# A recurrent branch run as four streams (direction x half of the heads) instead of two directions

## The reference, cut to what matters

```python
def step(s, inp):
    r_t, w_t, k_t, v_t, a_t, b_t = inp
    sa = jnp.einsum("bhvk,bhk->bhv", s, a_t)
    s = (s * w_t[:, :, None, :] + sa[..., None] * b_t[:, :, None, :]
         + v_t[..., None] * k_t[:, :, None, :])
    return s, jnp.einsum("bhvk,bhk->bhv", s, r_t)
...
for d in range(N_DIR):
    a_d = a[:, :, d]
    k_d = heads(k * (1 + (a_d - 1) * k_a))
    y_d, s_d = wkv_scan(rh, heads(decay[:, :, d]), k_d, vh, -kk, kk * heads(a_d),
                        s0[:, d].astype(f32), reverse=(d == 1))
```

## Time and profile before

| | us |
|---|---|
| median of 3 runs | 1853.98 (1853.29 to 1858.33) |
| span of the profiled execution (no other time of its own is given) | 1866.7 |
| PE matmul busy | 1767.0 (95%) |
| DVE busy | 1136.2 (61%) |
| ACT busy | 887.2 (48%) |
| POOL busy | 579.5 (31%) |

### The profile page before, as it was taken

The page is one execution under the profiler, slowest core; times in us unless marked ns, Lnnn a source line. Parts: engine busy times, 40 slices in busy tenths (PEclk is TensorE's granted clock), DMA queues, the critical chain, the costliest instruction groups (busy, mean ns, idle before and its releaser), DMA issues.

```text
span 1866.7 us, 40944 instructions
## 1 busy us (share of the span) xinstructions
PE 1767.0 (95%) x16496; PEld 1617.0 (87%) x16496; DVE 1136.2 (61%) x1650; ACT 887.2 (48%) x1338; POOL 579.5 (31%) x438
## 2 busy tenths in 40 slices
PE   7999989899999999999999799999989999999996
PEld 7888868799999999999888698999878888888885
DVE  1675657655222121004766787542499999999998
ACT  2562132153444334335532423433557777777775
POOL 1651000154666666565530002655510000000000
PEclk9999969999999999999999899999999999999998
DMA  8534241433443344343342500335579999999991
GB/s 283 172 102 148 94 139 54 151 99 104 136 124 105 122 136 134 125 120 102 91 136 90 178 26 22 119 101 161 203 250 345 335 348 338 331 329 325 326 342 45
DMA packets 226886, 321.62 MB, mean 172 GB/s; under 512 B 15798, under 2 KB 169780, under 8 KB 226612
## 3 DMA queue, kind: packets, MB, share of 16 engines
q1 hardware_dynamic: 220112, 308.26, 50.4%
q0 software_dynamic: 1728, 6.29, 0.9%
q10 hardware_dynamic: 4900, 4.93, 0.8%
HBM read 315.77 MB, written 3.67 MB: 171 GB/s over the span
## 4 chain that ended last, share of the span: by engine, by line
PE 76%; DVE 13%; issue 5%; ACT 2%; DMA 2%; POOL 1%; DVEq 1%; SPq 0%; ACTq 0%
PE bank L630 74%; DVE e_w_rest L189 4%; PE bank L627 2%; DMA ring<-in_w_ada 2%; DVE S L2103 2%; POOL weights_rest L2520 1%; DVE cvT L2052 1%; DVE yacc L2410 1%; DVE esig L2469 1%; ACT weights_rounded L1416 0%; ACT e_w_rounded L1453 0%; DVE U L2133 0%; DVE ey_rest L2424 0%; DVE St L2155 0%; DVE hT L1863 0%
## 5 line engine op out<-in xcount | busy, mean ns | idle before, releaser
L2520 POOL TENSOR_TENSOR weights_rest<-ring,weights_rounded 128x512 fp32r<-128x512 f32 x344 | 467.8, 1366 | 482.1 <-ACT weights_rounded L1416 481.8
L1416 ACT ACTIVATE weights_rounded<-ring 128x512 fp32r<-128x512 f32 x344 | 213.6, 629 | 332.7 <-PE bank L630 328.6
L1453 ACT ACTIVATE e_w_rounded<-e_raw 128x1024 fp32r<-128x1024 f32 (+1 forms) x327 | 315.7, 989 | 101.4 <-PE bank L630 96.2
L189 DVE TENSOR_TENSOR e_w_rest<-e_raw,e_w_rounded 128x1024 fp32r<-128x1024 f32 (+1 forms) x326 | 355.1, 1133 | 8.5 <-ACT e_w_rounded L1453 7.6
L630 PE MATMUL bank<-h_rounded,weights_rounded 128*128 128x384 f32 x688 | 235.7, 343 | 8.4 <-POOL weights_rest L2520 5.7
L630 PE MATMUL bank<-h_rounded,weights_rest 128*128 128x384 f32 x688 | 233.2, 339 | 0.0
L630 PE MATMUL bank<-h_rest,weights_rounded 128*128 128x384 f32 x688 | 232.0, 337 | 0.0
L630 PE MATMUL bank<-e_w_rounded,hG_rounded 128*128 128x512 f32 (+1 forms) x432 | 166.6, 386 | 13.0 <-DVE e_w_rest L189 6.9
L630 PE MATMUL bank<-e_w_rounded,hG_rest 128*128 128x512 f32 (+1 forms) x432 | 162.5, 376 | 0.0
L630 PE MATMUL bank<-e_w_rest,hG_rounded 128*128 128x512 f32 (+1 forms) x432 | 162.5, 376 | 0.0
L2603 POOL DMA_INDIRECT hgt<-h_rows,rows_at x9 | 13.6, 1515 | 449.1 <-DVE wnext L2439 449.1
(11 more groups left out here) (355 smaller groups left out, 3658.7 us busy)
## 6 DMA issues: line engine op xcount, KB each, us to landing
ring<-in_w_ada SPq DMA_DIRECT2D x96, 512.0 KB, 6.1
e_raw<-in_moe_w_down SPq DMA_DIRECT2D x90, 512.0 KB, 4.6
ring<-in_w_in SPq DMA_DIRECT2D x88, 512.0 KB, 4.6
e_raw<-in_moe_w_gate SPq DMA_DIRECT2D x72, 512.0 KB, 7.1
e_raw<-in_moe_w_up SPq DMA_DIRECT2D x72, 512.0 KB, 8.0
e_raw<-in_moe_w_gate SPq DMA_DIRECT2D x36, 384.0 KB, 6.4
e_raw<-in_moe_w_up SPq DMA_DIRECT2D x36, 384.0 KB, 4.3
ring<-in_ffn_w_gate SPq DMA_DIRECT2D x22, 512.0 KB, 4.8
```

What stands on the lines that cost most here:

```text
L189: eng.tensor_tensor(wl, e_raw[n % E_RAW][:, 0:kn * w], wr.bitcast(F32), ALU.subtract).then_inc(s("e_rest"), 1)
L1416: a(w_parts[n % NSLOT][0], raw, ACT.Copy).then_inc(*E.up("rounded_ready", *key))
L1453: a(e_w[n % E_PARTS][0][:, 0:kn * w], e_raw[n % E_RAW][:, 0:kn * w], ACT.Copy).then_inc(s("e_rounded"), 1)
L2520: pool.tensor_tensor(wl, raw, wr.bitcast(F32), ALU.subtract).then_inc(*E.up("rest_ready", *key))
```

## The change

The branch runs as four streams s = 2 d + g, where g is a half of the heads (heads 4 g to 4 g + 3, channel tiles 2 g and 2 g + 1).

- PE, ACT and DVE get a `scan` that takes work to run behind W, in front of the wait for U, and behind the step. Scan 0 carries the levels of stream 1; scan 1 the tokens, pairs, level 0 and levels 1 and 2 of stream 2; scan 2 the same of stream 3; scan 3 has ada halves and taps. The levels' units are now 8 and 4 blocks (`UNITS`), each with its own bank (3 and 7) and its own Xs.
- `low` products of direction 1 run between the levels of stream 0. Keys of direction 1 are prepared per half (`later_decay(g)`, `later_keys(g)`, `grown_keys(g)`, `later_queries(g)`, ACT's `later_exps(g)`).
- The state is kept without the zeros; products with it take one row half, then wait for PE's own semaphore, then the other (`with_state`). The two chunks of a step are updated by one add and one multiply over two neighbouring banks (`two`). `Sfin` is a slot of `St`.
- Outputs of a chunk pair follow as soon as its chunks are scanned (`done_pairs`).
- W and U share bank 0; there is one `Wb`.
- AR and BK no longer fit beside each other with both directions alive: BK lies over x, the decays of direction 1 (`incl1`, `excl1`) over h. x and h are written to DRAM at the head of the z stage by ACT's queue and read back in stream 3's last levels; DVE waits for them in front of BK, of the rest of h and of the residual.
- No `FILL` matmuls; `meanwhile` runs ada halves alone. Taps: 12 ahead of the first masks, the others as below.

```diff
+UNITS = ((0, 8), (8, 4))
...
                 def meanwhile(n):

                     for _ in range(n):
-                        if next(next_ada, None) is None:
-                            for _ in range(FILL):
-                                mm(psum[7][:, 0:P], ident, ident, True, True)
+                        next(next_ada, None)
...
+                def with_state(b, s_, cs, k):
+
+                    d, g = divmod(s_, 2)
+                    for hh in range(2):
+                        for mm_ in range(2):
+                            for c in cs:
+                                if c != starts(d)[0]:
+                                    hr = hh ^ (c % 2)
+                                    m, h4, r = 2 * g + mm_, 2 * mm_ + hr, quads[hr]
+                                    last = mm(b[quads[c % 2], h4 * C:(h4 + 1) * C], AR[r, m, c, k, :], St[r, c + 1, m, :],
+                                              False, hh == 1 and mm_ == 1)
+                        if hh == 0:
+                            last.then_inc(*E.step())
+                            pe.wait_ge(*E.latest())
+                    return last
...
+                def scan(s_, after_w, before_s, after_s):
+
+                    d = s_ // 2
+                    for i in range(len(steps(d))):
+                        step_w(s_, i)
+                        after_w[i]()
+                        step_u(s_, i)
+                        if nxt(d, steps(d)[i][-1]) is None:
+                            before_s[i]()
+                            pe.wait_ge(*drained("U", l, s_, i))
                         else:
...
+                            for part, _ in enumerate(step_s(s_, i)):
+                                if part == 0:
+                                    before_s[i]()
+                        if done_pairs(d)[i] is not None and i + 1 < len(steps(d)):
+                            outputs(s_, done_pairs(d)[i])
+                        after_s[i]()
...
+                level_d(0, 5)
+                meanwhile(1)
+                scan(0, [lambda lev=lev: level_x(1, lev) for lev in range(1, 5)], [lambda lev=lev: level_d(1, lev) for lev in range(1, 5)],
+                     [lambda: meanwhile(1), nothing, nothing, nothing])
+                level_x(1, 5)
+                ending(0)
+                level_d(1, 5)
...
+                    scan(s_ - 1, [keyed, lambda: pairs(s_, 1, (3, 7)), lambda: level_x(s_, 1), lambda: level_x(s_, 2)],
+                         [stated, nothing, lambda: level_d(s_, 1), lambda: level_d(s_, 2)],
+                         [paired, lambda: pairs(s_, 2, (3, 7)), nothing, nothing])
+                    level_x(s_, 3)
+                    ending(s_ - 1)
+                    level_d(s_, 3)
+                    for lev in (4, 5):
+                        meanwhile(1)
+                        level_x(s_, lev)
+                        meanwhile(1)
+                        level_d(s_, lev)
+                    meanwhile(3 - s_)
+                one = lambda: meanwhile(1)
+                scan(3, [one] * 4, [nothing] * 4, [one, one, nothing, nothing])
+                ending(3)
                 for _ in next_ada:
                     pass
-                meanwhile(3)
```

ACT, and DVE behind the first keys:

```diff
+                act.dma_start(x_keep, xT).then_inc(*E.up("x_kept", l, by=16))
+                act.dma_start(h_keep, hT).then_inc(*E.up("h_kept", l, by=16))
...
+                scan(0, [lambda lev=lev: squares_of(1, lev) for lev in range(1, 5)], [nothing] * 4,
+                     [lambda: key_gain(1, (0, 1)), lambda: (key_gain(1, (2, 3)), later_exps(0)), lambda: later_exps(1), nothing])
...
+                first_keys()
+                taps(12)
+                for cp in range(NCP):
+                    masks(0, cp)
+                level_0(0)
...
+                scan(0, [nothing] * 4,
+                     [lambda: (level(1, 1), later_decay(1)), lambda: (level(1, 2), later_keys(0)),
+                      lambda: (level(1, 3), grown_keys(0)), lambda: level(1, 4)])
+                level(1, 5)
+                for s_ in (2, 3):
+                    later_queries(s_ - 2)
+                    scan(s_ - 1, [nothing] * 4,
+                         [lambda: masks(s_, 0), lambda: (masks(s_, 1), masks(s_, 2), level_0(s_)),
+                          lambda: level(s_, 1), lambda: level(s_, 2)])
+                    level(s_, 3)
+                    outputs(s_ - 1, done_pairs(0 if s_ == 2 else 1)[-1])
+                    if s_ == 2:
+                        later_keys(1)
+                    else:
+                        taps(3)
+                    level(s_, 4)
+                    if s_ == 2:
+                        grown_keys(1)
+                    else:
+                        taps(3)
+                    level(s_, 5)
+                    taps(2)
+                scan(3, [nothing] * 4, [lambda: taps(4)] * 4)
+                taps(2 * CONV_W)
+                outputs(3, done_pairs(1)[-1])
+                dve.wait_ge(*E.latest())
+                dve.wait_ge(*at("h_back", l))
                 for g in range(4):
                     rest("gate", l, g, hT[:, 2 * g:2 * g + 2, :])
```

More of the change, by code:

```diff
@@ L18 @@
 C = 64
+NG = NH // 2
 NC_ = T // C
@@ L49 @@
 F32 = mybir.dt.float32
-FILL = 4
 F32R = mybir.dt.float32r
@@ new lines, in step_w @@
+                def step_w(s_, i):
+                    d, g = divmod(s_, 2)
+                    b = begin("W", l, s_, i, use=0)
+                    for h4 in range(NG):
+                        for c in steps(d)[i]:
+                            cp, q = chunk(c)
+                            h = NG * g + h4
+                            mm(b[q, h4 * C:(h4 + 1) * C], S1[q, nth(s_, cp, h4), 2 * C:3 * C], vtok[q, cp, h * C:(h + 1) * C],
+                               h4 == 0, c == starts(d)[0] and h4 == NG - 1)
+                    if i == 0:
+                        pe.wait_ge(*drained("s0", l, s_))
+                    else:
+                        pe.wait_ge(*drained("S", l, s_, i - 1, 0))
+                    with_state(b, s_, steps(d)[i], 0).then_inc(*E.fill("W", l, s_, i))
@@ new lines, in step_u @@
+                def step_u(s_, i):
+                    d = s_ // 2
+                    b = begin("U", l, s_, i, use=0)
+                    if i == 0:
+                        for w in range(len(UNITS)):
+                            pe.wait_ge(*drained("D", l, s_, LEVELS, w))
+                    for h4 in range(NG):
+                        for c in steps(d)[i]:
+                            cp, q = chunk(c)
+                            last = mm(b[q, h4 * C:(h4 + 1) * C], Tt[q, nth(s_, cp, h4), :], Wb[q, h4 * C:(h4 + 1) * C], True, True)
+                    last.then_inc(*E.fill("U", l, s_, i))
@@ new lines, in into_state @@
+                def into_state(s_, i, k, values, start):
+                    d, g = divmod(s_, 2)
+                    step = steps(d)[i]
+                    for mm_ in range(2):
+                        for hh in range(2):
+                            for j, c in enumerate(step):
+                                cp, q = chunk(c)
+                                hr = hh ^ (c % 2)
+                                h4 = 2 * mm_ + hr
+                                h = NG * g + h4
+                                last = mm(bank("S", l, s_, i, j)[quads[hr], mm_ * C:(mm_ + 1) * C], tok[q, k, cp, h * C:(h + 1) * C],
+                                          values(q, c, h4), start and mm_ == 0, not start and mm_ == 1)
+                                if not start and mm_ == 1 and hh == 1:
+                                    last.then_inc(*E.fill("S", l, s_, i, j))
@@ new lines, in _ @@
+                first_state(0, 2)
+                for cp in range(NCP):
+                    tokens(1, cp, (3, 7, 0)[cp])
+                first_state(1, 1)
+                pairs(1, 0, (2, 0))
+                level_x(0, 1)
+                meanwhile(1)
+                level_d(0, 1)
+                pairs(1, 1, (1, 2))
+                level_x(0, 2)
+                meanwhile(1)
+                level_d(0, 2)
+                pairs(1, 2, (0, 1))
+                level_x(0, 3)
+                low_product(1, 0, 0, use=2)
@@ L1638, in branch_rounded @@
+                scan(3, [nothing] * 4, [nothing] * 4, [nothing] * 4)
+                ending(3)
                 def branch_rounded(pos, src, g=0):
@@ new lines, in masks @@
+                def masks(s_, cp):
+                    d = s_ // 2
+                    for hr in range(2):
+                        dve.wait_ge(*filled("pair", l, s_, cp, hr))
+                        src = bank("pair", l, s_, cp, hr)[:, :].rearrange("p (h w) -> p h w", h=2)
+                        msk = pair_mask[:, d:d + 1, :].broadcast_to([P, 2, 256])
+                        h0 = nth(s_, cp, hr)
+                        tt(S1[:, h0:h0 + 3:2, :], src, msk, M).then_inc(*E.read("pair", l, s_, cp, hr))
@@ L2157, in _ @@
[L2157 to L2165 removed]
+                        dve.wait_ge(*filled("U", l, s_, i))
```

(14 more changed lines are left out.)

698 lines of the change are left out of this document (362 added, 336 removed).

## The result

The changed kernel takes **1899.16 us** (median of 4 runs, 1895.89 to 1901.13) against 1856.15 (4 runs, 1853.29 to 1867.05) of the kernel before: ratio 1.0211 [1.0184, 1.0238], 43 us slower. Forecast was 1842, 12 us faster, with a range to 1872.

What follows compares the result with a forecast made beforehand. TensorE bounds (76% of what ended last). Stage sums 184.1 and 181.7 us, plus DMA stalls and clock, became 192 and 187; -17 + 2.5 + 2 for spilling = -12, from the median 1853.98 to 1842; range 1820 to 1872.

Steps and rivals of the forecast that it cites:

- TensorE's work: Whole stage: matmuls priced from profile rows at full clock, such as 13.65 us per stream's inversion, 5.1 for low products.
- The base: Both stages: the first profile's 208.9 and 184.3 us, in a span of 1866.7, taken as the starting point.
- A difference of stages carries over: Whole kernel: the 12 us gained on the profiled span was also taken off the runs' median, 1853.98, giving 1842.
- The clock: Both stages: restarts after idling run at 1.2 GHz for some microseconds, costing 3 us in layer 0, 2 in layer 1.
- Rival D: After the idle tail: PE stays at half clock for 24 us, losing 12 us a layer, total 1861; chance 0.08.
- Stalls under DMA: Both stages: issue stalls during ada refills, which mostly stand alone; 5 us in layer 0, 3 in layer 1.
- The tail: After scan 3's last U copy: 28 taps on DVE take 15.2 us and set the end; PE idles some 13.
- The waits of scan 0: Scan 0: PE waits 1.7 us for a U copy, then 3.5 and 1.2 for W copies behind ACT's exps.
- step 1 of the sum: Up to the first scan step: transposes, pairs, initial states, one inversion, ada halves and low products take PE 33.4 us.
- The self-wait: State products: PE waits for its own semaphore between row halves, 0.25 us each, 28 a layer, 7 us.
- The spill: Writing x and h to DRAM at the z stage's head: 1 us a layer, 2 in all; reloads cost 0.
- Rival B: All scans: steps wait for W and U copies, 1 us more than allowed in each of 32, total 1874; chance 0.17.

Runs made afterwards that it cites:

- the re-laid kernel: Changed kernel with taps moved from the tail, ada halves spread, x and h reloaded earlier, then taps and halves re-placed against new waits: 1855.11 us, ratio 0.9962.
- three good moves: Changed kernel with 27 taps moved from behind the last steps, ada halves spread, and x and h reloaded earlier, all together: 1879.98 us, ratio 1.0106.

## Why the prediction was wrong

The miss is 57 us: 39.3 between the profile that the sum gave (1854.7) and the one measured (1894.0), and 17.8 because the measured median lies 5.2 above its profile's span where I had subtracted 12.7.

Two steps of the prediction failed in their mechanism. The ada halves were taken to stand apart, with 8 us for all stalls and 5 for the clock; in fact they are bunched, which costs the re-laid kernel 30.0 us (spreading three of four alone gave the changed kernel 13.6). And the loss of one execution was taken for a property of the kernel before; a second profile is 12.9 us shorter in the stages. The two prices were measured from different kernels, so they don't add up exactly.

Laid beside the sum by pieces, ahead of scan 3 (the rows of the table above without the last; idle and lost clock cut at the pieces' ends):

| us | forecast | layer 0 | layer 1 |
|---|---|---|---|
| TensorE's work at full clock | 138.0 | 143.2 | 142.8 |
| idle | 10.4 | 17.0 | 17.6 |
| lost clock | in the 5 for both layers | 10.1 | 7.1 |

Scan 3 and the tail came out 10.6 us above the sum in layer 0 (4.6 lost clock, and waits for the ring of 2.42 and 3.09) and 2.0 in layer 1.

- **The base.** "A difference of stages carries over" failed. The 12.7 us by which the span stood above the runs was itself a sign that this execution had lost something that the others had not, and the earlier trace rows showed where: clock 0.77 in the first scan. I counted it as something to win. In the second profile the clock is low for 4 us there instead of 24, and the stage is 191.92. The forecast for layer 0, 192, was no gain at all. With the second profile as its base, the same sum would have come out as no change.
- **The clock** (3 and 2 us): measured 15.3 and 13.1 lost. This is the term that was mis-sized most. Rival D named a long stretch at half clock, at the wrong place: behind the idle tail there was little to lose (2 us). It came in scans 2 and 3, and the sign that I had given for D, clock 0.5 inside the scans, is the one that came true. D's price of 12 us a layer was near the 14.7 and 12.4 measured, by luck, since its place was wrong; I gave it a chance of 0.08.
- **Stalls under DMA** (5 and 3 us): "each ada refill now mostly stands alone" is wrong by the diff itself: four halves stand in levels 4 and 5 of streams 2 and 3 and a fifth behind stream 2's, five in 12 us. Idle time put down to "issue" or to the ring is 12.6 and 4.1 us in the two layers (1.67 of the first stands where the sum had a wait for U). Putting the halves back like this costs the re-laid kernel 30.0 us, clock included.
- **The tail** was right: 28 taps, 14.89 us for 15.2, PE idle 10.8 and 12.7 for 13. The runs price it at 15.6 to 21.2 us. It was in the sum, and so is no part of the miss.
- **The waits of scan 0** were right: 3.27 and 3.45 for 3.5; 1.01 and 1.00 for 1.2; and 1.56 for 1.7 where a copy of U is late in layer 1.
- **TensorE's work** was priced 3.0 us too low up to scan 0, where the engine is busy all the time at clock 1.00, and 5 us a layer up to scan 3. (The items of step 1 of the sum add up to 33.3, where it says 33.4.) A part of the inversion takes 1.54 instead of 1.41, the eight low products about 6 instead of 5.1. The rows show that it depends on what follows:

```profile
174.18 1.55 PE L651 MATMUL bank<-Xs,Tt 64*64 64x64 f32 x45
175.52 0.32 PE L651 MATMUL bank<-AR,BK 64*64 64x128 f32 x1
175.52 0.28 PE L651 MATMUL bank<-Xs,Tt 64*64 64x64 f32 x3
...
188.34 1.61 PE L651 MATMUL bank<-inv,S 64*64 64x64 f32 x48
189.88 0.91 PE L651 MATMUL bank<-z,low 64*128 64x384 f32 x2
```

  D at 174.18 is followed 1.34 us later by pairs, which have the same tile shape, and three of its 48 matmuls start beside them; X at 188.34 is followed 1.54 us later by products of another shape, and the one low product at 189.88 takes 0.84 where 0.64 were priced. So 0.1 to 0.2 of the 0.2 that I took off each row come back at each change of shape, and the change puts ada halves and low products between X and D. The rule that I cited for the 64x64 products (the Trainium skill, "TensorEngine Tiling (Array Packing)", Key Properties: a change of tiling mode drains the engine) agrees with this trace, and should have been used here.
- **The self-wait** (0.25) was right: 0.22 to 0.28. **The spill** (2 us) fits: 2.2 us, with an interval that takes in nothing and up to 6.
- **Rival B** (steps wait for their copies) is false: of the 16 steps of layer 0, two wait over 1 us for W, none for U; in layer 1 one waits for U as well.

What stays open is the link from a wait to the length of the low clock. That bunching the halves costs time, and brings the long stretch at the head of scan 2, is shown by putting it in and taking it out. Whether the refills do it or the new places of the matmuls isn't separated: no kernel ran bunched products without their refills. Full DMA engines are not needed for low clock: behind the wait of 3.27 us for ScalarE's copy at 219.11, with a DMA share of 0.02 ahead of it, the clock is 0.50 for some 3 us, and the 20 us and 10 us shown above follow waits of 1.18 and 0.76 us with a DMA share under 0.1 just ahead. Why the same wait is followed by full clock, by 4 us or by 10 to 20 us at half clock isn't shown.

## What to carry to other kernels

Work that brings its own DMA traffic is not free cover: spread it, and look at how close the pieces stand, not at how many a stage holds. If a profile's span lies above the median of its runs, find what that execution lost before taking the difference as a gain, and profile the kernel a second time. And try moves together: here three good moves gave 19 of 32 us until the waits that they made for each other were mended.

## What the runs showed of the hardware

- TensorE stayed at 1.2 GHz for 10 us with 9.94 of them busy (1093 to 1103 in the changed kernel), and for 14 us with 13.84 busy. The Trainium skill, "TensorE: Matmul & The Clock Gate", Part 1, says that activity releases the throttle. The stretches that ended after some 4 us agree; in these two TensorE stayed throttled although the profile shows it busy.
- The same kernel, the same stall: 2.30 us in the earlier trace rows was followed by some 24 us of low clock, 2.70 us in the second profile by 4. A wait of 0.76 us at the head of scan 1 was followed by 10 us of half clock in one execution and by none in another.
- Twelve and six matmuls of the identity in the idle places of a scan changed its lost clock from 3.0 to 3.2 us and lengthened it by 5.1.
- Runs of the kernel before lay between 1849.1 and 1874.7 us over the sessions. With ten runs of a kernel against 13 to 19 of that one, the interval of a ratio was still 0.14 to 0.28% to either side.
